# Ten adaLN modulation units moved from TensorE's weight ring to column tiles on VectorE, one or two more places for the experts' down matrices, and row spreads as transposes

## What is computed

```
sh1, sc1, g1, sh2, sc2, g2 = split(silu(c) @ w_ada + b_ada, 6)      # w_ada 1024 x 6144 per layer, c and c_ctx
h  = rms_norm(x) * (1 + sc1) + sh1
qa, ka, va, qd, kd, vd, glu, gates = project(h @ w_in)
y  = sig(g0)*(attend(qa,ka,va) @ w_o_mla) + sig(g1)*(conv(glu) @ w_o_conv) + sig(g2)*(diff(qd,kd,vd) @ w_o_diff)
x  = x + g1 * (y @ w_out)
h2 = rms_norm(x) * (1 + sc2) + sh2
x  = x + g2 * sum over 2 of 32 experts of w * ((silu(h2 @ w_gate[e]) * (h2 @ w_up[e])) @ w_down[e])
```

## Time and profile before

| | |
|---|---|
| median of 3 runs | 1501.93 us (1501.10 to 1503.51) |
| time of the profiled execution | 1503.67 us |
| its span | 1501.9 us |
| TensorE busy | 1414.6 us (94%) |
| VectorE, ScalarE, GpSimd busy | 740.5, 371.4, 173.8 us |
| HBM read | 346.57 MB |
| mean granted TensorE clock | 0.985 |

### The profile page before, as it was taken

One profiled execution on the slowest core, in us unless ns is written; L12 is line 12 of the kernel. 1 busy time (PEld: TensorE's weight loads), 2 busy tenths in 40 slices (PEclk: granted clock), 3 DMA queues, 4 the chain that ended last, 5 costly groups with the idle time before them and its releaser, 6 DMA issues.

```text
span 1501.9 us, 19322 instructions
## 1 busy us (share of the span) xinstructions
PE 1414.6 (94%) x7630; PEld 811.2 (54%) x7630; DVE 740.5 (49%) x1644; ACT 371.4 (25%) x807; POOL 173.8 (12%) x118
## 2 busy tenths in 40 slices
PE   6999999999999999989997879999999999999786
PEld 3444344554454445655544437654677886666553
DVE  2579944558566953533211117795454443444232
ACT  4112414532222012312221125240543203000001
POOL 0021421000011210012222110143000110000000
PEclk9999999999999999999999999999999999999998
DMA  9312331134322446289999988531223468999996
GB/s 389 143 60 106 149 117 51 57 137 144 125 99 112 153 196 252 110 335 418 418 418 421 417 349 353 220 113 57 82 101 141 167 251 331 403 420 420 421 420 264
DMA packets 52494, 350.79 MB, mean 234 GB/s; under 512 B 8116, under 2 KB 8628, under 8 KB 20144
## 3 DMA queue, kind: packets, MB, share of 16 engines
q1 hardware_dynamic: 46800, 338.99, 56.5%
q0 software_dynamic: 5024, 8.40, 1.5%
q10 hardware_dynamic: 576, 2.10, 0.3%
HBM read 346.57 MB, written 11.80 MB: 239 GB/s over the span
## 4 chain that ended last, share of the span: by engine, by line
PE 78%; SPq 8%; DMA 7%; DVE 3%; ACT 2%; issue 1%; DVEq 0%; ACTq 0%
PE bank L418 74%; DMA arena<-w_up_in 6%; SPq L2813 4%; ACT arena L1243 2%; SPq L2802 2%; SPq L2822 2%; PE bank L764 2%; DMA arena<-ada_in 1%; PE bank L518 1%; PE bank L1131 1%; DVE arena L1703 1%; DMA x<-x_in 0%; PE bank L1151 0%; DVE am L1989 0%; PE bank L886 0%
## 5 line engine op out<-in xcount | busy, mean ns | idle before, releaser
L418 PE MATMUL bank<-arena 128*128 128x512 f32 (+10 forms) x6104 | 1253.0, 448 | 46.2 <-DMA arena<-w_up_in 39.7
L418 PEld LDWEIGHTS bank<-arena 128*128 128x128 f32 (+4 forms) x6104 | 666.3, 160 | 537.0 <-issue 407.9
L1243 ACT ACTIVATE arena<-bank 128x512 f32<-128x512 f32 (+5 forms) x431 | 206.8, 498 | 949.3 <-PE bank L418 846.2
L1703 DVE SCALAR_TENSOR_TENSOR arena<-arena,bank 64x256 f32<-64x256 f32 (+2 forms) x121 | 57.9, 479 | 309.7 <-ACT arena L1243 227.4
L1703 DVE SCALAR_TENSOR_TENSOR arena<-arena,vec 128x512 f32<-128x512 f32 (+1 forms) x254 | 175.6, 764 | 0.4
L1989 DVE TENSOR_REDUCE am<-bank 128x1 f32<-128x512 f32 (+1 forms) x96 | 55.5, 599 | 166.1 <-PE bank L418 166.0
L2608 POOL TENSOR_TENSOR arena<-arena 128x512 f32<-128x512 f32 (+1 forms) x32 | 37.4, 1169 | 434.9 <-DVE arena L1703 434.9
L1243 ACT ACTIVATE arena<-bank,am 128x512 f32<-128x512 f32 (+1 forms) x96 | 58.6, 613 | 75.7 <-DVE am L1992 75.5
L2647 POOL DMA_INDIRECT y<-arena,routing x33 | 33.0, 999 | 183.9 <-ACT arena L1243 183.9
L764 PEld LDWEIGHTS bank<-con,arena 128*128 128x128 f32 x240 | 29.8, 141 | 34.4 <-issue 21.6
L2051 DVE SCALAR_TENSOR_TENSOR arena<-arena 128x1024 f32<-128x1024 f32 x32 | 44.4, 1401 | 6.1 <-DMA arena<-adaT_in 6.1
(11 more groups left out here) (193 smaller groups left out, 766.0 us busy)
## 6 DMA issues: line engine op xcount, KB each, us to landing
arena<-w_down_in SPq DMA_DIRECT2D x65, 1024.0 KB, 20.3
arena<-w_gate_in SPq DMA_DIRECT2D x61, 1024.0 KB
arena<-w_up_in SPq DMA_DIRECT2D x61, 1024.0 KB
arena<-ada_in SPq DMA_DIRECT2D x12, 2048.0 KB, 11.0
arena<-mg_in SPq DMA_DIRECT2D x12, 2048.0 KB, 8.2
arena<-adaT_in SPq DMA_DIRECT2D x16, 1024.0 KB, 7.2
arena<-mo_in SPq DMA_DIRECT2D x6, 2048.0 KB, 8.5
arena<-glu_in SPq DMA_DIRECT2D x4, 2048.0 KB, 17.8
```

The lines of the kernel that those rows point to most:

```text
L418: return nc.tensor.matmul(out, w, rhs, start=start, stop=stop)
L1243: return nc.scalar.activation(out, in_, fn, **kw)
L1703: return V.scalar_tensor_tensor(out, in0, sc, in1, op0=op0, op1=op1)
```

## The change

- `COLUMN_UNITS`: layer 0 has seven column units (4 to 10, 28 tiles), layer 1 has three (6 to 8, 12 tiles). The six ring units that ran inside the projections are gone. Tiles of layer 0 still begin at u = 25, one per step. In steps 32 to 47 (`COLUMN_PAIRS`) a second tile follows at the end of the step, behind the branches, so that the 28 tiles end in step 42. Layer 1 has one tile in each of the steps 1 to 12.
- SP's order of loads follows: tiles 9 to 15 behind `mo1`, 16 to 23 behind `mg4`, 24 to 27 ahead of `mo2` in layer 0, in layer 1 tiles 0 to 8 behind `mo0` and 9 to 11 behind `mg2`.
- Down matrices have seven places in layer 0 and eight in layer 1 (`NDOWN`), one of them a new tile, `down_more`, of 8 KB per partition (the scratch for GpSimd's DMA descriptors is set to 8192). In layer 0 `w_down` 0 is loaded with the first gate and up matrices, 4 no longer waits for the router, 6 is loaded ahead of the loop. In layer 1 `w_down` 0 and 4 are loaded before the stage of the experts, 6 and 7 ahead of the loop, and from then on each pair's down matrices one pair earlier, except the last pair's. `final_g` is loaded behind the last expert instead of ahead of the second half of `w_out`.
- `spread_rows` (`g1` of both layers, `g2` of layer 0) and `row_of` use transposes. `g2` of layer 0 is spread at expert 31 instead of between the layers, and the unit between the layers is taken on VectorE behind the first norm.

```diff
-COLUMN_UNITS = ((4, 5, 6, 7), ())
+COLUMN_UNITS = ((4, 5, 6, 7, 8, 9, 10), (6, 7, 8))
+COLUMN_PAIRS = (range(32, 48), ())
+NDOWN = (7, 8)
...
-                    [arena[:, c:c + 2048] for c in (8192, 18672, 10240, 4096, 6144, 16384)])
+                    [c if not isinstance(c, int) else arena[:, c:c + 2048]
+                     for c in ((down_more, 18672, 10240, 4096, 6144, 16384, 8192),
+                               (down_more, 18672, 10240, 4096, x[:, 0:2, :].rearrange("p t d -> p (t d)"), 16384, 8192, 6144))[l]])
...
-                if kind in (("dq", "ukv", "dk"), ("glu", "lora"))[l]:
+                if kind in ((), ())[l]:
                     units += more[:1]
...
-                            last = mm(ps[:, 128 * k:128 * k + 128],
-                                      src[:, c0 + 4 * half + k, v:v + 1].to_broadcast([128, 128]), ident, True, True)
+                            last = nc.tensor.transpose(ps[:, 128 * k:128 * k + 128],
+                                                       src[:, c0 + 4 * half + k, v:v + 1].to_broadcast([128, 128]), ident)
...
+                    if e == NB[l] - 2:
+                        pe.wait_ge(s["xgt_ready"], NB[l])
+                        pools["a"] = (2, 3)
+                        spread_rows(l, "g2", ada[l], 5 * KD, TOK)
...
                     if u >= 1:
                         out_d(u - 1)
                     merge_tiles(nA + u, None if u else 1)
+                    if nA + u in COLUMN_PAIRS[l]:
+                        ada_column(nA + u)
...
-                    ada_evac(units[between[0]])
                     mixed(0, 2, 0)
                     mixed(0, 3, 1, lambda: row_rstd(S[1], 0))
                     row_half(S[1], 0, 2)
+                    ada_evac(units[between[0]])
...
-                    for unit_, first, end in (("mg3", 0, 9), ("mo1", 9, 13), ("mg4", 13, 16)) if l == 0 else (("mo0", 0, 9), ("mg2", 9, 12)):
+                    for unit_, first, end in (("mg3", 0, 9), ("mo1", 9, 16), ("mg4", 16, 24)) if l == 0 else (("mo0", 0, 9), ("mg2", 9, 12)):
...
                 def expert_wd(e):
-                    j = e % NSLOT
-                    if e >= NSLOT:
-                        sp.wait_ge(s["y_full"], blocks_before(e))
+                    j = down_slot(l, e)
+                    if e >= NDOWN[l]:
+                        sp.wait_ge(s["y_full"], e - NDOWN[0] + 1 if l == 0 else (e - NDOWN[1]) // 2 + 1)
...
+                if l == 1:
+                    expert_wd(0)
...
+                if l == 1:
+                    expert_wd(4)
```

More of the change, by code:

```diff
@@ L196, in build @@
         gu_ready = [sem(f"gu_ready{j}") for j in range(NSLOT)]
-        wd_ready = [sem(f"wd_ready{j}") for j in range(NSLOT)]
+        wd_ready = [sem(f"wd_ready{j}") for j in range(NDOWN[1])]
         quarter_ready = [[sem(f"quarter_ready{b}_{q}") for q in range(1, 4)] for b in range(2)]
@@ L281, in loads_of_slot, with down_slot, downs_of_slot @@
             return e // NSLOT + 1 + l * len(range(e % NSLOT, NB[0], NSLOT))
+        def down_slot(l, e):
+            return e % NDOWN[l]
+        def downs_of_slot(l, e):
+            return e // NDOWN[l] + 1 + (len(range(down_slot(1, e), NB[0], NDOWN[0])) if l and down_slot(1, e) < NDOWN[0] else 0)
         def wait_apart(eng, sm, value):
@@ L950, in row_of @@
                             for t in range(2):
-                                last = mm(ps[:, 256 * m + 128 * t:256 * m + 128 * t + 128], cols(m, t).to_broadcast([128, 128]), ident, True, True)
+                                last = nc.tensor.transpose(ps[:, 256 * m + 128 * t:256 * m + 128 * t + 128],
+                                                           cols(m, t).to_broadcast([128, 128]), ident)
                         end("d", last)
@@ L2070, in ada_column @@
                 def ada_column(u):
-                    k, n_ = u - COLUMN_FROM[l], len(columns[l])
-                    if n_ and k == -1:
+                    n_ = len(columns[l])
+                    if n_ and u == COLUMN_FROM[l] - 1:
                         silu()
+                    if not n_ or u < COLUMN_FROM[l]:
+                        return
+                    k = next_column[0]
+                    next_column[0] += 1
                     if 0 <= k < n_:
@@ L2852, in _ @@
                 if l == 0:
-                    for e in range(NSLOT, NE + 1):
-                        if e < NE:
-                            expert_gu(e)
-                        if e > NSLOT:
-                            expert_wd(e - 1)
-                else:
+                    expert_wd(6)
+                    for e in range(NSLOT, NE):
+                        expert_gu(e)
+                        if e >= NDOWN[0]:
+                            expert_wd(e)
+                else:
+                    expert_wd(6)
+                    expert_wd(7)
                     for e in range(NSLOT, NE, 2):
@@ L2861, in _, with block_loads @@
                         expert_gu(e + 1)
-                        expert_wd(e)
-                        expert_wd(e + 1)
+                        for e_ in (e + 2, e + 3) if e + 4 < NE else (e, e + 1) if e + 2 == NE else ():
+                            expert_wd(e_)
+                    sp.wait_ge(s["gu_full"], NPAIR - 1)
+                    sp.dma_start(fing, a["final_g"].to_broadcast([128, D])).then_inc(fing_loaded, 16)
                 sp.wait_ge(s["over_tables"], seen(l, "over_tables", 1))
                 X0 = NB[l] - NE
-                def block_loads(j):
+                def block_loads(j, to=2):
                     e = sp.value_load(meta[l][0:1, bass.ds(j, 1)], min_val=0, max_val=NE - 1)
```

85 lines of the change are left out of this document (43 added, 42 removed).

## The result

The changed kernel takes 1493.62 us (median of 4 runs, 1492.65 to 1494.76), the one before 1502.47 us on the same chip. The ratio is 0.9940, with an interval from 0.9926 to 0.9954: 8.85 us faster, where 14.3 were forecast. The profiled execution is the shortest of the four: 1492.65 us, its span 1490.7, so 11.2 under the span of before.

What follows compares the result with a forecast made beforehand. TensorE (78% of the chain of waits) and the experts' loads by DMA (15%) were taken to bound the kernel in turns. Nine terms, gains less the attention's +7.9 and +1.9, summed to -14.3, so 1487.6 us, range 1477 to 1497.

Steps and rivals of the forecast that it cites:

- the two terms of the down places: Experts' stages: extra down places load bytes before the full DMA stretch, shortening it by 2.5 us (layer 0) and 5.0 (layer 1).
- Ring units: Projections: each of three ring units per layer costs 2.20 us, so removing them gains 6.6 us in each layer.
- Tiles in layer 0: Attention of layer 0: second tiles are free until step 40, then VectorE's lag makes TensorE wait, +7.9 us.
- wrong altogether: Two signs: VectorE waits for the tiles' loads, or the clock, 1.00 in the projections, falls where TensorE now waits.
- Rival B: Attention: TensorE has other work while VectorE catches up, so both attention terms vanish: 1477.8 us, chance 0.15.
- rival D: Attention: VectorE becomes the bound and every tile in pair steps and layer 1 is paid for: 1519.8 us, chance 0.05.
- The three terms of 1.0 for GpSimd: Attention of layer 0, steps 40 to 42: one product per step runs beside a GpSimd addition, 1.0 us longer each.
- Tiles in layer 1: Attention of layer 1: most of 12 tiles are free; two steps cost 1.2 us, the first tile's load 0.7: +1.9.
- Spreads: Ahead of the output projection: spreading `g1` by transposes gains 1.3 us in layer 0 and 0.3 in layer 1.
- Between the layers: `mixed` waited behind the unit's evacuation on VectorE; moving that behind it starts `mixed` 1.8 us sooner.
- Rival C: Experts: down places buy nothing, as six gate and up places hold the queue back: 1495.1 us, chance 0.19.
- Item 4 of the prediction: The spreads' item; it also said the `g2` spread at expert 31 has DMA time to hide in.

Runs made afterwards that it cites:

- ring_l1: The changed kernel with layer 1's three ring units back behind glu and lora and no column tiles in layer 1's attention: 1499.64 us, ratio 0.9975 to the kernel before.
- tiles_later: The changed kernel with no column tile in steps 41 to 43 of layer 0, the last four in steps 44 to 47, `mo2` loaded ahead: 1486.84 us.
- hybrid: The changed kernel with down matrices loaded one expert (layer 0) or one pair (layer 1) later from expert 26 and 24 on: 1489.00 us, ratio 0.9906.
- evac_first: The changed kernel with the evacuation of the unit between the layers ahead of `mixed` on VectorE again: 1493.43 us, ratio 0.9930 to the kernel before.
- late_down: The changed kernel with its extra down places, but SP's earlier load order in the full DMA stretch put back: 1492.04 us, ratio 0.9917 to the kernel before.
- spreads_matmul: The changed kernel with `spread_rows` and `row_of` as matmuls again, `g2` of layer 0 still at expert 31: 1494.23 us, ratio 0.9942 to the kernel before.
- after_again: A second series of the changed kernel, file unchanged: 1495.06 us, ratio 0.9952 to the kernel before.
- best: hybrid with column tiles placed as in tiles_later, but the last two behind layer 0's attention: 1484.79 us, ratio 0.9880 to the kernel before.
- best_b: The same as best with only one column tile behind layer 0's attention: 1483.27 us, ratio 0.9868 to the kernel before.

## Why the prediction came out as it did

The direction was right and 1493.6 lies in the range. The size was not: -8.9 for -14.3. That it came no worse is partly luck. In the ledger the two terms of the down places miss by 8.6 us; of the other differences, 5.9 us go the other way, among them 2.9 that no term had (1.0 ahead of the projections, 1.9 ahead of the first expert).

1. **Ring units: right, mis-sized in layer 0.** 7.8 for three where 6.6 was taken, so 2.6 each for 2.20. In layer 1 it was 6.8 and 7.2, 2.3 to 2.4 each, and ring_l1 gives 4.6 for the net of the units and their tiles. The unit's own rows have the 2.20, so the rest lies outside them; where, I did not test.
2. **Tiles in layer 0: right, step by step.** 7.2 for 7.9, with each of the three times within 0.7 us, and tiles_later removes it. One sign of being "wrong altogether" did come: the clock fell where TensorE waits (0.72 from 435 to 440). In the change it cost little beyond VectorE's lag, in two other traces 2.8 us more (last section). The other sign did not: VectorE waited twice for a tile's load (5.5 us in all, the second one at 394.8), but the stretch had lost nothing when step 41 began. Rival B (covered) and rival D (a stall in every pair step) fall: the pairs of steps 32 to 39 left 2.46 idle at step 40. The three terms of 1.0 for GpSimd were two, 1.06 each. "Nothing" for `mo2`, issued 14 us later in the forecast, holds: it lands 10.5 us after its issue at 445.76, and no wait of TensorE names it.
3. **Tiles in layer 1: the size right, the parts only in one step.** +2.4 and +2.9 for +1.9. The step with the convolution's reciprocal is one place. VectorE's 3.4 us of convolution work come ahead of the maximum, and TensorE's turn, which waited 0.54 in the earlier trace rows, waits 1.68:

```profile
1080.53 0.66 PE L778 MATMUL bank<-con,arena 128*128 128x128 f32 x4 [1.68 <-DVE arena L2023]
```

```profile
1084.00:1086.00 2.00, 2.00 (x6) 1.62 (x6) 0.90 (x3) 1.97 (x6) 0.00 (x0) 0.57 0.35 112
```

   That is the 1.2 of one step. The 0.7 for the first tile is not there: TensorE had lost nothing until this turn. The other 1.2 are matmuls behind it at a granted clock of 0.57. Eight other traces with these tiles have +1.3 or +1.4 for the whole stretch, near the one wait alone; hybrid has +2.4.

4. **Spreads: right.** -1.2 for -1.3, -0.7 for -0.3.
5. **Between the layers: the size right (-2.3 for -1.8), the cause wrong.** I gave it to the evacuation's new place behind `mixed`. evac_first shows that this is worth nothing once the spread is gone. From the first load of `y` to `mixed` it is 4.9 us, not the 3.6 of a single load. And the spread did not vanish: it takes 2.4 us at expert 31 now, about what its leaving gave here.
6. **The down places: the step that failed** (5 and 7: -2.5 and -5.0, measured -0.3 to -0.8 and +1.4 to -0.4). I counted the bytes that move into idle DMA time, and they do: DMA ended 15.3 us earlier in layer 1, 3.1 beyond the stage's own gain (of 5.0 forecast). But TensorE does not wait for the end of DMA. It waits for one up matrix, and the change puts each pair's down matrices a pair earlier, so two more stand ahead of that matrix. 2.1 MB ahead of it cost what 2.1 MB moved away had brought. Rival C had said that "the bytes only change their order" and gave 1495.1, which is nearer than my forecast; its condition (six gate and up places hold the queue back) is half of it, as late_down's idle DMA shows. In layer 0 neither place nor order showed a gain: -0.3 and -0.8 in the change, +0.2 in late_down. Item 4 of the prediction had the spread of `g2` at expert 31 hide in DMA time, and there the trace contradicts it. Before, TensorE waited for weights near the stage's end; in the change its last wait for weights there is the 0.20 ahead of 862.64, and the spread comes after that.

```profile
880.37 1.08 PE L418 MATMUL bank<-arena 128*64 128x256 f32 x8 [2.26 <-DMA arena<-w_up_in]
```

```profile
862.64 5.39 PE L432 MATMUL bank<-arena 128*64 128x256 f32 x40 [0.20 <-DMA arena<-w_up_in]
```

   The spread's 2.4 us are the size of what is missing there (2.2), but no run leaves it out, so its share stays open.
7. **Not forecast:** 0.9 to 1.9 us ahead of the first expert. spreads_matmul has it too, so it isn't the transposes. TensorE's transposes ahead of the first expert took 1.87 before and 1.04 now; the granted clock was 0.50 to 0.61 there before (651 to 655) and 0.80 now (648 to 650). What brings the clock back there I didn't try.

The times of single runs spread widely in the change (1491.3 to 1499.0 in after_again). The last section shows what may be one source of it.

## What to carry to other kernels

In a stage that is bound by DMA, look at what the waiting engine waits for and count the bytes that stand ahead of it and behind it in the queue: a place more is worth its bytes only if they aren't put ahead of the awaited load. Load the less urgent matrices early while DMA would idle, and late once it is full: that was worth 6 us against the change (hybrid), 1.7 us by the ratios against the plain late order of late_down, and 1.0 to 2.9 on top of tiles_later (best, best_b), of which only the first is clear of the noise. With the order of before the two extra places were worth less than could be measured (0.8 us by the medians, 2.0 by the ratios). And work that is put on a following engine is free up to its idle time ahead of each hand-over: write that idle time down step by step and stop at the step where it ends, here step 40.

## What the runs showed of the hardware

**VectorE and GpSimd take turns, whole instructions long.** At 428.10 GpSimd's addition starts beside a product that runs until 429.16. It takes 2.18 instead of 1.27, until 430.28, and the next product, started at 429.08, takes 2.28 instead of 1.22. Both lose: the addition 0.9, the product 1.06. The same pair of numbers stands at 438.43 (with GpSimd's addition of 437.45). The earlier trace rows has the 2.28 at 549.29, and the addition beside it, at 548.31, took 2.18 too. The Trainium skill ("SBUF — State Buffer", section "SBUF: two separate sides") says that one of the two has the shared ports for a whole instruction while the other blocks, and this trace agrees: 430.28 plus the 1.1 of a product is 431.4, where the next maximum starts (431.37).

**TensorE's clock fell behind waits of 1.3 to 2.1 us, and where it fell decided the price.** In two of the eight traces with the change's tile places (hybrid, evac_first) the attention of layer 0 lost 10.0 us instead of 7.2. TensorE and a window of hybrid, and the same window of the change:

```profile
438.46 1.97 PE L432 MATMUL bank<-arena 128*128 128x128 f32 x7 [1.30 <-DVE arena L2037]
...
444.62 0.66 PE L778 MATMUL bank<-con,arena 128*128 128x128 f32 x4 [2.04 <-DVE arena L1722]
...
447.20 3.75 PE L432 MATMUL bank<-arena 128*128 128x128 f32 x10 [1.30 <-DVE arena L2037]
449.04 5.49 PE L432 MATMUL bank<-arena 128*128 128x512 f32 x8
...
449.00:451.00 2.00, 2.00 (x5) 0.97 (x4) 1.18 (x5) 1.02 (x4) 0.00 (x0) 0.50 1.01 426
```

```profile
449.00:451.00 2.00, 2.00 (x9) 0.77 (x7) 0.69 (x1) 0.38 (x1) 0.00 (x0) 1.00 1.15 492
```

The rows of hybrid at 447.20 and 449.04 are of two windows and overlap. In the change the clock fell behind the first two waits, in a step in which VectorE sets the pace: TensorE was slower there and waited 0.35 instead of 2.04 at the next turn, so most of it cost nothing more. In hybrid it stayed up there and fell two waits later, to 0.50 (1.2 GHz), when VectorE had caught up and TensorE had the work: 8 records of 512 columns take 5.49, 0.69 each, where the earlier trace rows has 0.43. The turn behind them is 2.8 us later. Nothing in this part of the program tells the change and evac_first apart, so a kernel with such waits can spread in time. That this is a source of the spread of after_again is likely, not shown: one execution of it is in a trace, and that one lost 7.2.
